# Fourteen gate and up units of both convolution parts by seven products, with merged joins

## The reference

```python
gate = h2 @ w_gate; up = h2 @ w_up
x = x + (silu(gate) * up) @ w_down            # first network, width 2816

u = h @ w_up                                   # second, 2 x 2816 columns
c = conv(u, conv_w, padding=[(2, 0)], groups=u.shape[-1]) + conv_b
g, val = jnp.split(c, 2, axis=-1)
x = x + (silu(g) * val) @ w_down
```

## Time and profile before

| | us |
|---|---|
| median of 3 runs | 1713.62 (1712.62 to 1713.7) |
| the profiled execution | 1712.91 |
| its span | 1711.1 |
| TensorE busy | 1700.8 (99%) |
| VectorE busy | 1278.1 (75%) |
| ScalarE busy | 864.3 (51%) |
| GpSimd busy | 361.6 (21%) |

### The profile page before, as it was taken

The page is one execution under the profiler, slowest core; times in us unless marked ns, Lnnn a source line. Parts: engine busy times, 40 slices in busy tenths (PEclk is TensorE's granted clock), DMA queues, the critical chain, the costliest instruction groups (busy, mean ns, idle before and its releaser), DMA issues.

```text
span 1711.1 us, 24883 instructions
## 1 busy us (share of the span) xinstructions
PE 1700.8 (99%) x9596; PEld 1476.2 (86%) x9596; DVE 1278.1 (75%) x1968; ACT 864.3 (51%) x1530; POOL 361.6 (21%) x264
## 2 busy tenths in 40 slices
PE   9999999999999999999999999999999999999998
PEld 8888888998998888888888988889898888898897
DVE  5789656897696846695979966755889687996575
ACT  5554533443354646554545533547877454454354
POOL 2003204442325011102144202022110213520200
PEclk9999999999999999999999999999999999999999
DMA  5212333334222221213233341323111234334122
GB/s 173 74 62 72 99 99 124 99 99 146 77 75 87 62 82 57 73 51 98 88 134 111 99 123 50 90 74 93 40 50 50 87 95 127 99 99 136 62 87 74
DMA packets 125196, 152.90 MB, mean 89 GB/s; under 512 B 7526, under 2 KB 96904, under 8 KB 125080
## 3 DMA queue, kind: packets, MB, share of 16 engines
q1 hardware_dynamic: 124776, 150.99, 27.9%
q10 hardware_dynamic: 304, 0.33, 0.1%
HBM read 148.61 MB, written 2.10 MB: 88 GB/s over the span
## 4 chain that ended last, share of the span: by engine, by line
PE 94%; DVE 4%; POOL 1%; issue 1%; ACT 1%; DVEq 0%; ACTq 0%; POOLq 0%
PE bk L2422 23%; PE bk L2424 23%; PE bk L2423 23%; PE bk L2464 5%; PE bk L2466 5%; PE bk L2465 5%; PE bk L2427 4%; PE bk L2569 2%; DVE FS L2624 1%; POOL FS L3011 1%; PE bk L2603 1%; PE bk L2530 1%; PE bk L2602 1%; DVE WL L2636 1%; PE bk L2557 1%
## 5 line engine op out<-in xcount | busy, mean ns | idle before, releaser
L2422 PE MATMUL bk<-R,WH 128*128 128x512 f32 (+1 forms) x1394 | 521.2, 374 | 0.9 <-DVE WL L2636 0.7
L2424 PE MATMUL bk<-R,WL 128*128 128x512 f32 (+1 forms) x1394 | 515.0, 369 | 0.0
L2423 PE MATMUL bk<-R,WH 128*128 128x512 f32 (+1 forms) x1394 | 514.8, 369 | 0.0
L2636 DVE TENSOR_TENSOR WL<-RAW,WH 128x1024 fp32r<-128x1024 f32 (+5 forms) x198 | 248.2, 1255 | 153.5 <-ACT WH L2861 152.3
L2861 ACT ACTIVATE WH<-RAW 128x1024 fp32r<-128x1024 f32 (+5 forms) x198 | 202.8, 1026 | 213.8 <-PE bk L2424 152.5
L2422 PEld LDWEIGHTS bk<-R,WH 128*128 128x128 f32 x1394 | 263.0, 189 | 45.3 <-DVE WL L2636 2.1
L2424 PEld LDWEIGHTS bk<-R,WL 128*128 128x128 f32 x1394 | 262.8, 189 | 44.9
L2423 PEld LDWEIGHTS bk<-R,WH 128*128 128x128 f32 x1394 | 263.2, 189 | 41.0
L3007 POOL TENSOR_TENSOR OVER<-TOK 128x1024 f32<-128x1024 f32 x28 | 76.3, 2725 | 382.0 <-DVE WL L2633 216.4
L2464 PE MATMUL bk<-WH,R 128*128 128x512 f32 (+4 forms) x394 | 144.7, 367 | 0.0
L2466 PE MATMUL bk<-WL,R 128*128 128x512 f32 (+4 forms) x394 | 139.3, 353 | 0.0
(11 more groups left out here) (235 smaller groups left out, 3251.8 us busy)
## 6 DMA issues: line engine op xcount, KB each, us to landing
RAW<-in_ffn_w_down_dram SPq DMA_DIRECT2D x44, 512.0 KB, 3.9
RAW<-in_ffn_w_up_dram SPq DMA_DIRECT2D x64, 256.0 KB, 3.0
TOK<-in_ffn_w_up_dram SPq DMA_DIRECT2D x14, 1024.0 KB, 5.1
RAW<-in_ffn_w_up_dram SPq DMA_DIRECT2D x28, 512.0 KB, 3.6
RAW<-in_w_down_dram SPq DMA_DIRECT2D x22, 512.0 KB, 3.6
RAW<-in_da_w_qkv_dram SPq DMA_DIRECT2D x32, 256.0 KB, 3.0
TOK<-in_w_gate_dram SPq DMA_DIRECT2D x7, 1024.0 KB, 5.4
TOK<-in_w_up_dram SPq DMA_DIRECT2D x7, 1024.0 KB, 5.0
```

The lines of the kernel that those rows point to most:

```text
L2422: e.matmul(dst, lh, rh, start=start, stop=False)
L2423: e.matmul(dst, lh, rl, start=False, stop=False)
L2424: return e.matmul(dst, ll, rh, start=False, stop=stop)
L2636: e.tensor_tensor(low, sides(st.n, raw_home(st.n)), high.bitcast(F32), ALU.subtract).then_inc(on["wlo_dve"], 1)
```

## The change

The up units of blocks 4 to 10 of both convolution layers are done by seven products as well. The seven joins of a unit become four (three of them over 512 columns), with a second copy by ScalarE; two pairs of products share a bank. In convolution layers the low half of one of a unit's four chunks (number 1, n3) is no longer made by VectorE: ScalarE writes minus the high half, and a transfer that GpSimd issues adds the values from OVER to it. The partial sums of the activations are kept in PART instead of FS slots, and their makers get rank 1.5 until the products of the part's blocks are issued, then 0.5.

```diff
-PARTS = (range(0, 4), range(4, 8), range(8, 11))
-SEVENS = ({fb: (0, 2) for fb in range(4, 11)}, {fb: (0,) for fb in range(4, 11)}, {fb: (0,) for fb in range(4, 11)})
+THIRDS = (range(0, 4), range(4, 8), range(8, 11))
+BLOCKS = (THIRDS, THIRDS, THIRDS)
+SEVENS = ({fb: (0, 2) for fb in range(4, 11)}, {fb: (0, 2) for fb in range(4, 11)}, {fb: (0, 2) for fb in range(4, 11)})
+EARLY = -2
+MARGIN = (3, 5, 5)
+RANKS = (1.5, 0.5)
+ADDED = ((), (1,), (1,))
+NADD = 4
...
+                if kind == "wadd":
+                    free_at[eng] = begins(eng, fields["after"]) + 1000.0
+                    ready_at[id(fields["done"][0]), fields["done"][1]] = free_at[eng] + 3000.0
+                    continue
...
-                lo = w_low[n] = yield step("wlo", n=n, m=chunks[n][0] * chunks[n][1], after=[st.act])
+                if n in sevens and sevens[n][1] in ADDED[layer_of(n)]:
+                    k = adds[0]
+                    adds[0] += 1
+                    done = s_add[k % NADD], 16 * (k // NADD + 1)
+                    st = yield step("wneg", n=n, m=chunks[n][0] * chunks[n][1], after=[st.act])
+                    lo = yield step("wadd", n=n, done=done, after=[st.act, (done[0], done[1] - 16)] if k >= NADD else [st.act])
+                    lo.dve = done
+                    w_low[n] = lo
+                else:
+                    lo = w_low[n] = yield step("wlo", n=n, m=chunks[n][0] * chunks[n][1], after=[st.act])
...
-                for kp in range(4):
-                    spawn(self.make(kp), 0.5)
+                N.uses += 4
+                self.makers = [spawn(self.make(kp), RANKS[0]) for kp in range(4)]
...
-                while kp and self.own[kp - 1] is None:
+                while kp and (self.own[kp - 1] is None or ("s4", kp - 1) not in self.of):
...
-                e, o, p, q = slots = [fsl.get() for _ in range(4)]
-                E, O, A, B = (FS[:, s.i, 0:S] for s in slots)
+                e, o = fsl.get(), fsl.get()
+                E, O = (FS[:, s.i, 0:S] for s in (e, o))
+                A, B = PART
...
             def middle():
...
+                while q.first is None or len(fsl.fr) < 2:
+                    yield None
+                l, r = sorted((fsl.get(), fsl.get()), key=lambda s: s.i)
+                right = FS[:, r.i, 0:S]
+                st = yield step("join", dst=FS[:, l.i:r.i + 1:r.i - l.i, 0:256], src=halves_of(b2), x=one.unsqueeze(1).to_broadcast([P, 2, 256]),
+                                op=ALU.add, after=counts([done6, q.first, l.free, r.free]))
+                put_bank(b2, st.dve)
+                part_free[u % 2] = [st.dve]
+                third = yield step("join", dst=right[:, 256:S], src=BK[b7.i][:, 0:256], x=right[:, 0:256], op=ALU.add, after=counts([done7, st.dve]))
+                put_bank(b7, third.dve)
+                copied = yield step("keep", dst=FS[:, l.i, 256:S], src=right[:, 256:S], after=counts([third.dve, l.free]))
+                st = yield step("join", dst=right.rearrange("p (x c) -> p x c", x=2), src=BK[b5.i][:, 0:256].unsqueeze(1).to_broadcast([P, 2, 256]),
+                                x=right.rearrange("p (x c) -> p x c", x=2), op=ALU.subtract, after=counts([done5, third.dve, copied.act]))
+                put_bank(b5, st.dve)
+                q.low, q.both = [copied.act, st.dve], (l, r)
...
+            def outer():
...
+                l, r = q.both
+                at_l = FS[:, l.i, 256:S]
+                both = bass.AP(at_l.tensor, at_l.offset, [at_l.ap[0], [FW * (r.i - l.i) - 256, 2], [1, 256]])
+                st = yield step("join", dst=both, src=halves_of(b4), x=both, op=ALU.add, after=counts([done3, q.low]))
+                put_bank(b4, st.dve)
+                spawn(ev(0, l, st.dve), 0)
+                spawn(ev(1, r, st.dve), 0)
...
+                elif k == "wneg":
...
+                    e.activation(four(st.n, home(st.n)[1]), of_unit(st.n), ACT.Copy, scale=-1.0).then_inc(on["wneg_act"], 1)
...
+                elif k == "wadd":
...
+                    o = 2 * S * (sevens[st.n][1] - 1)
+                    e.dma_start(home(st.n)[1], OVER[:, o:o + 2 * S], accum_op=ALU.add).then_inc(st.done[0], 16)
```

More of the change, by code:

```diff
@@ L258, in build @@
         s_unit = [sem(f"s_unit{i}") for i in range(2)]
+        s_add = [sem(f"s_add{i}") for i in range(NADD)]
         FLAT = [t.rearrange("p t c -> p (t c)") for t in TOKS]
@@ L502, in plan_ffn @@
                 zones[layer] = [len(chunks), len(chunks), len(units)]
-            for fb in PARTS[part]:
+            parts = BLOCKS[layer]
+            for fb in parts[part]:
                 sevenfold = SEVENS[layer].get(fb, ())
@@ L534, in build @@
         plan_rows(w_out, 512, 4)
-        for part in range(len(PARTS)):
+        for part in range(len(BLOCKS[0])):
             plan_ffn(part, ((w_gate, 0), (w_up, 0)), w_down)
@@ L546, in build @@
         plan_last_rows(da_o, 768)
-        for part in range(len(PARTS)):
+        for part in range(len(BLOCKS[1])):
             plan_ffn(part, ((up2[0], 0), (up2[0], 2816)), dn2[0])
@@ L610, in home, with layer_of @@
             return KFLAT[:, o:o + m], KFLAT[:, o + SLOT:o + SLOT + m]
+        def layer_of(n):
+            return next(i for i, z in enumerate(zones) if z and z[0] <= n < z[1])
         def of_unit(n):
@@ L1700, in seven @@
             q = Group()
-            q.first = q.second = q.third = q.left = q.right = q.y = None
-            one, two = PART[u % 2][:, 0:256], PART[u % 2][:, 256:S]
+            q.first = q.low = q.both = None
+            one = PART[u % 2][:, 0:256]
             def split(n):
@@ L1708, in split, with product @@
                 return w_low[n].dve
-            def product(n, half, name):
-                b = yield from bank("gemm")
-                st = yield step("piece", n=n, half=half, xs=X.operand(name), bank=b.i, after=counts([w_low[n].dve, X.ready, b.free]))
+            def product(n, half, name, b=None, o=0):
+                if b is None:
+                    b = yield from bank("gemm")
+                st = yield step("piece", n=n, half=half, xs=X.operand(name), bank=b.i, o=o, after=counts([w_low[n].dve, X.ready, b.free]))
                 if half or n == n2:
@@ L1723, in seven, with first @@
             yield from split(n1)
[L1724 to L1728, removed]
+            b1, done1 = yield from product(n1, 0, "a11")
+            def first():
+                st = yield step("keep", dst=one, src=BK[b1.i][:, 0:256], after=counts([done1, part_free[u % 2]]))
+                put_bank(b1, st.act)
                 q.first = st.act
[L1731 to L1742, removed]
+            spawn(first(), 0)
+            b2, _ = yield from product(n1, 1, "a12")
             yield from split(n3)
@@ L1746, in seven @@
             yield from split(n4)
-            b6, done6 = yield from product(n4, 0, "s2")
+            _, done6 = yield from product(n4, 0, "s2", b2, 256)
             def middle():
-                while q.first is None:
+                while q.first is None or len(fsl.fr) < 2:
                     yield None
-                q.second = yield from join(two, b6, done6, one, ALU.add, q.first, part_free[u % 2])
-                put_bank(b6, q.second)
-                while q.left is None:
-                    yield None
[L1756 to L1777, removed]
@@ new lines, in middle @@
+                put_bank(b5, st.dve)
+                q.low, q.both = [copied.act, st.dve], (l, r)
+            spawn(middle(), 0)
+            b4, _ = yield from product(n4, 1, "a22")
+            yield from split(n2)
+            _, done3 = yield from product(n2, 0, "s4", b4, 256)
+            X.over(done3)
+            def outer():
+                while q.both is None:
+                    yield None
+                l, r = q.both
[5 more added lines that the diff above has]
+                spawn(ev(1, r, st.dve), 0)
@@ L1794, in ffn @@
                 opened[0] = hi
-            for part in range(len(PARTS)):
-                Gt, last, held = [], part == len(PARTS) - 1, None
-                for fb in PARTS[part]:
+            parts = BLOCKS[layer]
+            for part in range(len(parts)):
+                Gt, last, held = [], part == len(parts) - 1, None
+                for fb in parts[part]:
                     pairs, keep = [Pair(), Pair()], {}
                     Gt += pairs
-                    if zone and part == 0 and fb == PARTS[0][-2]:
-                        held = Combined(N, counts(ptfree), counts(kfree[4 + 4 * NSK:]))
+                    if zone and part == 0 and fb == parts[0][EARLY]:
+                        part_free[0], part_free[1] = counts(tok_users), counts(tok_users)
+                        held = Combined(N, counts(ptfree), counts(kfree[4 + 4 * NSK:]), MARGIN[layer])
                     if X is None:
@@ L1820, in ffn @@
                     X.freed = N.shut = True
+                    for s in X.makers:
+                        s.rank = (RANKS[1], s.rank[1])
                 if last:
```

71 lines of the change are left out of this document (34 added, 37 removed).

## The result

The changed kernel takes 1756.7 us (median of 4 runs, 1754.6 to 1758.25) against 1713.34 before: ratio 1.0253, interval 1.0235 to 1.0271. It is slower by 43 us, where 1706.4 was forecast and the range ended at 1720. The profiled execution took 1758.25 us, its span 1756.4.

The account below looks back on a forecast made before the run. The prediction took TensorE's stream of columns as the bound, VectorE next. 1712.9 us less 11.2 gained on TensorE plus 4 of new waits gave 1705.7; with 0.7 for the median, 1706.4 us, range 1701 to 1720.

Parts of the forecast that it names:

- The gain on TensorE: Convolution up units by seven products: 84 matmuls in 10.1 us, 0.8 us saved a unit, 11.2 us over 14 units.
- VectorE's bill and the stretch: Convolution parts: VectorE needs 8.9 us a unit plus 3.0 to 3.9 stretch from GpSimd's sums, against TensorE's 10.1.
- What covers it: Convolution stages: 18 us cover against 14 to 22 short, 14 against 11 to 16; 4 us new wait in all.
- The end: Cover at the down product after eight units: its last pair is needed 9.5 us after the last low half starts.
- The first network: Its VectorE is short too, 10.5 us a unit against 10.1, and TensorE does not wait there.
- The transfer: n3's low half in convolution units: issue 1 us, landing 5, chain 10.5 us against a unit of 10.1; worth 0.
- Rival A: Convolution parts: VectorE and GpSimd become the bound because lateness cover is unusable; slower, priced at 1717 us, chance 0.13.
- The makers: Makers of the activations' partial sums, run later at lower rank: taken as 0, kept at 0 to 2 us a layer.

Follow-up runs that it names:

- e13: The changed kernel, transfers and order kept, with GpSimd's weight sums left out and constant fills of about their length in their place; 1700.6 us (0.9926).
- e5: e1 with GpSimd's weight sums left out and constant fills, made 2.5 times as long, written in their place; 1703.7 us (0.9943).
- e6: e1 with VectorE's two taps for each row block of a convolution part cut to their first 16 columns; 1709.6 us (0.9977).
- e14: e1 with a constant fill of the same length replacing only the first weight sum of each unit; 1716.1 us (1.0015).
- e1: The changed kernel without the adding transfer, all low halves made by VectorE again; 1751.9 us (1.0226).
- e12: e7 without the adding transfers; 1757.5 us (1.0259).
- e7: The changed kernel, transfer kept, with all weight sums of the units done by VectorE instead of GpSimd; 1766.5 us (1.0316).
- e8: e7 with a second low half of each convolution unit (n4's) made by ScalarE's negated copy and an adding transfer; 1839.7 us (1.0736).
- e3: The changed kernel with a unit's two later weight sums put behind its adding transfer in GpSimd's list; 1791.2 us (1.0452).
- e11: e1 with only planner estimates changed: VectorE instructions with two SBUF inputs charged the whole rest of GpSimd's running instruction; 1789.5 us (1.0441).
- e2: The changed kernel with the convolution parts' up units by eight products as before and no adding transfer; 1712.4 us (0.9994).

## Why the prediction was wrong

**The gain on TensorE** was right: with the port free the changed kernel has 84 matmuls in 10.1 us throughout (80.6 us for eight units) and takes 1700.6, 12.9 us less than the kernel before beside it, against 11.2.

**VectorE's bill and the stretch** were right. Joins take 0.685 us against 0.68. e13 has the changed kernel's lists without GpSimd's reading: VectorE is busy 66.9 us in its stage of eight units, 90.9 in the changed kernel. The bill has to be read behind the start of a stage, since VectorE has less to do until the first results come. The first two units of a stage and the other six, before (first network), then in the changed kernel:

```profile
320.20:340.40 20.20, 20.20 (x170) 20.20 (x169) 15.02 (x22) 9.32 (x12) 7.66 (x4) 1.00 0.26 87
340.40:401.10 60.70, 60.64 (x505) 60.43 (x505) 60.60 (x72) 28.83 (x40) 31.10 (x18) 1.00 0.28 88
```

```profile
916.20:936.20 20.00, 20.00 (x168) 20.00 (x167) 14.37 (x14) 12.58 (x17) 12.14 (x8) 1.00 0.51 134
936.20:1014.60 78.40, 67.39 (x506) 66.37 (x505) 76.53 (x79) 45.11 (x65) 40.05 (x23) 0.91 0.45 123
```

Six units took 76.5 us of VectorE, 12.8 each, the upper end of the 11.9 to 12.8 billed. In e13 the same six took 54.3, 9.0 each against 8.9 billed; the stretch is the difference, 3.7 a unit, billed at 3.0 to 3.9. The shortage was there as forecast.

**What covers it** is the step that failed. I added up 18 and 14 us of cover a stage, of which 5.3 and 6.8 were VectorE's idle time. The rows above show where that time lies: 5.2 of the 5.3 us in the first two units, ahead of the shortage. In the changed kernel 5.6 us stand idle in the same place. It was never cover. The end, put at 9.5 us, gave some 3.5: the last low half of a result starts 9.9 us into the down product, against 6.4 in the first network. And TensorE waited for the low halves of weights; slack at the end, in the results, does not help these. The first network was indeed full, 60.6 of 60.7 us of VectorE in six units without a wait of TensorE; but that shows cover for lateness of a few us (0.4 us a unit by my bill), not for 2.7 a unit. In the changed kernel TensorE waits for the first time 36 us into the stage.

From the third unit on, the longer of two times is what a stage takes, TensorE's 60.5 us for six units or VectorE's work:

| | VectorE busy, us | six units, us |
|---|---|---|
| e5 | 56.1 | 60.4 |
| e6 | 62.7 | 63.7 |
| e14 | 66.5 | 66.9 |
| changed kernel | 76.5 | 78.4 |
| e1 | 77.0 | 77.1 |

The four stages lie 50 us over their matmuls, where the forecast had 4. With no cover at all, the shortages as forecast give 1713.6 - 11.2 + 2 x (14 + 11) = 1752 at their low end and 1778 at their high end; 1756.7 was measured. e12, e7, e8, e3 and e11 are not on this line: VectorE is busy there in 70.9 of 75.7, 67.1 of 74.1, 65.0 of 99.8, 73.7 of 90.2 and 79.1 of 85.4 us, and presumably the order of the steps or the chain of the transfer costs more. That low halves of weights can be at most five chunks ahead, in the same list as the late taps, fits the waits of e1, most of them at low halves, but was not isolated.

**The transfer** was priced right in its parts (issue 0.88 us against 1, landing 4.5 after issue against 5) and wrong in its place: I let it run beside the later sums, and it stood behind them. That made 11.0 us in place of 10.5, harmless alone (e13).

**Rival A** had the outcome and, among its signs, the waits at VectorE's low halves, but a price of 1717, since it kept 8.5 and 9.2 us of cover, idle time included; with the high shortage and the same cover it had 1743. **The clock** was left out of the forecast. Its 16 us are part of how the 50 us look on TensorE; in e1, where VectorE is busy in 77.0 of the last 77.1 us, a faster TensorE would by this only have waited longer. What it cost by itself stays open.

The makers, the merged joins and the shared banks cost nothing, as forecast (e2).

## What to carry to other kernels

Before idle time of an engine is used as cover, look at where in the stage it lies: idle time ahead of the shortage covers nothing. Read an engine's busy time unit by unit; an average over a stage with an idle start makes a full engine look free. Where an engine's own list feeds the bound engine through few buffers, take the longer of the two engines' times behind the start of a stage. Moving work to an engine that reads the same memory port can cost the first engine more than the work, here some 23 us of VectorE's time a stage against 15.9: look for stretched rows of its two-input instructions, and take the reading away (a fill in its place) to see the whole price in one run.

## What the runs showed of the hardware

- GpSimd's writes into SBUF do not stretch VectorE (taps of 748 ns beside fills in e5), its reads do (1490 ns in the changed kernel): 48 us between e1 and e5. It agrees with the Trainium skill ("SBUF — State Buffer", section "Who interferes with whom"), which the prediction named. The taps are instructions with a scalar from memory beside two tensors, and are stretched like the low halves (1215 and 2490 ns).
- A transfer from SBUF to SBUF that adds, 512 KB issued by GpSimd, takes 0.87 us of its queue and lands 4.5 us after issue, beside 3.7 for a plain load of that size from HBM:

```profile
KT<-OVER POOLq DMA_DIRECT2D x14, 512.0 KB, 4.5
```

- TensorE's granted clock fell to 1.2 GHz after a single wait of 3.6 us, with matmuls 0.21 us apart until it rose again.
